# Rows of the first expert pair picked by matmul instead of gathered, in a one-core trunk kernel

## The reference

```python
h = h + moe(rms_norm(h, norm_ffn[i]), ...)
# moe, t = (512, 1024)
g_logits = t @ wg + bg                       # 4 groups
group = argmax(g_logits); p_group = softmax(g_logits)[group]
e_logits = (t @ we + be).reshape(-1, 4, 8)   # 32 experts
top_val, top_idx = top_k(e_logits[group], 2)
gate = softmax(top_val) * p_group            # on the two chosen experts, 0 elsewhere
hid = silu(t @ w1[e]) * (t @ w3[e]) * gate[e]
y  += hid @ w2[e]
```

## Time and profile before

| | |
|---|---|
| median of 3 runs | 1679.25 us (1678.71 to 1692.91) |
| the profiled execution | 1684.34 us |
| its span in the trace | 1682.5 us |
| mean granted clock of PE | 0.966 of full speed |
| busy: PE, DVE, ACT, POOL | 1522.7, 802.8, 419.4, 162.1 us |

### The profile page before, as it was taken

How to read it: one execution, slowest core, us unless ns; L and a number is a source line. 1 busy time by engine, 2 the same in 40 slices (tenths; PEclk the granted TensorE clock), 3 DMA queues, 4 the chain that set the end, 5 groups by cost and what they waited for, 6 DMA issues and landing times.

```text
span 1682.5 us, 29007 instructions
## 1 busy us (share of the span) xinstructions
PE 1522.7 (91%) x12509; PEld 934.8 (56%) x12509; DVE 802.8 (48%) x1403; ACT 419.4 (25%) x849; POOL 162.1 (10%) x183
## 2 busy tenths in 40 slices
PE   6999998889999999699887899999999997988886
PEld 4786777777644864433332378746558545333232
DVE  7655555553754445543221356446643544432125
ACT  2124255454301131400000120027421323000002
POOL 2000223231000000011111200000000001111001
PEclk9999999999999999799999999999999997999898
DMA  8208200011541521579999922220034234999995
GB/s 277 100 1 287 82 4 5 4 48 35 200 150 50 200 100 54 206 295 424 424 425 425 352 84 100 100 100 1 1 128 176 99 114 155 396 425 424 425 407 203
DMA packets 82338, 315.04 MB, mean 187 GB/s; under 512 B 17968, under 2 KB 19048, under 8 KB 57312
## 3 DMA queue, kind: packets, MB, share of 16 engines
q1 hardware_dynamic: 70112, 284.86, 43.6%
q0 software_dynamic: 10944, 24.10, 3.9%
q10 hardware_dynamic: 1152, 4.19, 0.6%
HBM read 306.86 MB, written 34.34 MB: 203 GB/s over the span
## 4 chain that ended last, share of the span: by engine, by line
PE 72%; DMA 14%; DVE 5%; ACT 3%; issue 3%; SPq 2%; PEld 0%; ACTq 0%; DVEq 0%; POOLq 0%
PE PS L790 20%; PE PS L657 13%; DMA arena<-in_moe_w 11%; PE PS L1442 9%; PE PS L2743 7%; PE PS L2768 5%; PE PS L1836 2%; PE PS L1772 2%; PE PS L2692 2%; PE PS L628 2%; PE PS L1812 1%; DMA ring<-in_moe_w 1%; PE PS L2097 1%; PE PS L2118 1%; PE PS L552 1%
## 5 line engine op out<-in xcount | busy, mean ns | idle before, releaser
L790 PE MATMUL PS<-arena,ring 128*128 128x256 f32 x1344 | 299.5, 383 | 2.8 <-DVE arena L934 2.8
L790 PEld LDWEIGHTS PS<-arena,ring 128*128 128x128 f32 x1344 | 255.6, 192 | 42.3 <-issue 6.3
L2743 PE MATMUL PS<-arena 128*64 128x512 f32 x704 | 166.4, 628 | 24.9 <-DMA arena<-in_moe_w 24.9
L657 PE MATMUL PS<-ring,arena 128*128 128x512 f32 x400 | 179.9, 596 | 0.7 <-ACT arena L2063 0.7
L2743 PEld LDWEIGHTS PS<-arena 128*64 128x64 f32 x704 | 52.6, 144 | 136.2 <-issue 103.3
L657 PEld LDWEIGHTS PS<-ring,arena 128*128 128x128 f32 x400 | 74.6, 192 | 83.3 <-issue 82.3
L2751 DVE TENSOR_TENSOR arena<-PS,arena 128x256 f32<-128x256 f32 x32 | 13.6, 424 | 218.6 <-PE PS L2758 201.3
L2748 ACT ACTIVATE arena<-PS 128x256 f32<-128x256 f32 x32 | 12.3, 383 | 327.7 <-PE PS L2743 327.7
L2743 PE MATMUL PS<-ring,arena 128*64 128x512 f32 x320 | 77.0, 637 | 16.1 <-DMA ring<-in_moe_w 12.9
L839 DVE TENSOR_TENSOR arena<-arena,PS 128x512 f32<-128x512 f32 x56 | 36.8, 684 | 112.4 <-PE PS L790 112.4
L1442 PE MATMUL PS<-ring 64*64 64x64 f32 (+1 forms) x3072 | 77.4, 234 | 10.6 <-issue 9.4
(11 more groups left out here) (336 smaller groups left out, 2219.0 us busy)
## 6 DMA issues: line engine op xcount, KB each, us to landing
arena<-in_moe_w SPq DMA_DIRECT2D x120, 1024.0 KB, 20.0
ring<-in_moe_w SPq DMA_DIRECT2D x72, 1024.0 KB, 17.6
ring<-in_sb_wqkv SPq DMA_DIRECT2D x6, 2048.0 KB, 9.2
ring<-in_xa_wq SPq DMA_DIRECT2D x4, 2048.0 KB, 8.6
ring<-in_xa_wo SPq DMA_DIRECT2D x4, 2048.0 KB, 14.2
ring<-in_xa_wkv SPq DMA_DIRECT2D x3, 2048.0 KB, 10.3
h<-in_x SPq DMA_DIRECT2D x8, 512.0 KB, 8.9
ring<-in_rw_wr SPq DMA_DIRECT2D x2, 2048.0 KB, 11.4
```

Of the source, the lines that this page charges most:

```text
L657: ins = pe.matmul(PS[:, BANK_OF[g], :], rows(k), cols[:, k, :], start=(k == 0 and not grows), stop=(k == 3), skip_group_check=grows)
L790: ins = pe.matmul(PS[:, BANK_OF[g], M * c:M * c + M], rows[:, k, o:o + P], cols[:, k, :], start=(c + k == 0 and not grows), stop=(k == 3), ...
L2743: ins = pe.matmul(bank(2, 2, F)[r, :, :], xgT[p][:, k, r], w[a][:, :, k, :], start=(k == 0), stop=(k == KC - 1))
```

## The change

Pair 0's rows are no longer gathered. For each token tile t a 128x128 matrix `picks[t]` is made, one-hot over pair 0's slots and scaled by the token's `rstd`: two `tensor_scalar` and one add. PE multiplies the residual tile `h[:, t, k::KC]` by it, 8 times for the 8 blocks of channels (`pick_tile`), and adds the four tiles up in banks 0 and 3: this gives the rows of pair 0 already turned. DVE scales them into `xgT[0]` (`xgT_first`). POOL makes `picks` for tiles 0, 1 and 2 (`pick_rows`), DVE for tile 3 within `place(3)`. POOL's memsets stand between its tiles 0 and 1. `place(1)` is moved ahead of `second(2)` on DVE. The table is finished later: `filled_table` of tiles 1 to 3 stands between the two halves of `up` of pair 0. POOL's gathers begin with pair 1.

```diff
+            pick_tile(pe, l, 0)
             late_turn(pe, ffn, NT - 1, ready, range(3))
             route_logits(pe, l, NT - 1, ahead)
...
+        def pick_tile(pe, l, t, ks=range(KC)):
+            if t < NT - 1:
+                pe.wait_ge(S("first_picks"), 14 * l + (4, 10, 14)[t])
+            else:
+                pe.wait_ge(S("first_rows"), 3 * l + 1)
+            for k in ks:
+                ins = pe.matmul(bank(PICK_BANKS[k // 4], 4, P)[:, k % 4, :], h[:, t, k::KC], picks[t % 3][:, 0, :],
+                                start=(t == 0 and k % 4 == 0), stop=True, ...)
...
         def moe_route_pe(pe, l):
-            for t in range(NT - 1):
-                filled_table(t)
+            filled_table(pe, l, 0)
+            pick_tile(pe, l, 1)
+            pick_tile(pe, l, 2)
             route_ranks(pe, l, NT - 1)
-            filled_table(NT - 1).then_inc(S("tabled"), 1)
+            pick_tile(pe, l, NT - 1, range(KC // 2)).then_inc(S("first_rows"), 1)
+            for p in range(2):
+                pe.nop().then_inc(S(f"xg_free{p}"), 1)
+            pick_tile(pe, l, NT - 1, range(KC // 2, KC)).then_inc(S("xg_free0"), 1)
+
+        def rest_of_table_pe(pe, l):
+            for t in range(1, NT - 1):
+                filled_table(pe, l, t)
+            filled_table(pe, l, NT - 1).then_inc(S("tabled"), 1)
...
# place(t), on DVE, ahead of OS
+                if t == NT - 1:
+                    own = picks[t % 3]
+                    for k in range(2):
+                        do(vec.tensor_scalar(own[:, k, :], iob, s8[:, NT * k + t:NT * k + t + 1], w_pick[:, k, t:t + 1],
+                                             ALU.is_equal, ALU.mult))
+                    vec.tensor_tensor(own[:, 0, :], own[:, 0, :], own[:, 1, :], ALU.add).then_inc(S("first_rows"), 1)
...
+            place(1)
             second(2)
-            place(1)
             place(2)
...
# POOL
+            def pick_rows(t, before):
+                b, own = 14 * l + before, picks[t]
+                pool.wait_ge(S("onehots"), 28 * l + (4, 6, 9)[t])
+                pool.tensor_scalar(w_pick[:, :, t], OB[:, t, :, 0], rstd[:, t:t + 1], None, ALU.mult)\
+                    .then_inc(S("first_picks"), 1)
+                pool.wait_ge(S("first_picks"), b + 1)
+                for k in range(2):
+                    m = NT * k + t
+                    pool.tensor_scalar(own[:, k, :], iob, s8[:, m:m + 1], w_pick[:, k, t:t + 1], ALU.is_equal, ALU.mult)\
+                        .then_inc(S("first_picks"), 1)
+                pool.wait_ge(S("first_picks"), b + 3)
+                pool.tensor_tensor(own[:, 0, :], own[:, 0, :], own[:, 1, :], ALU.add).then_inc(S("first_picks"), 1)
...
-            for n in range(4):
+            for n in range(1, 4):
                 fetch(n)
...
         def moe_pe(pe, l):
...
                 if n == 0:
-                    pe.wait_ge(S("first_rows"), 2 * l + 2)
+                    pe.wait_ge(S("first_rows"), 3 * l + 3)
                     up(pe, p, 2, w, range(KC // 2))
+                    rest_of_table_pe(pe, l)
                 pe.wait_ge(S("xgT_ready"), NPE * l + n + 1)
...
-            pe.wait_ge(S("table_ready"), l + 1)
-            for p in range(2):
-                pe.nop().then_inc(S(f"xg_free{p}"), 1)
-            turn(0)
```

More of the change, by code:

```diff
@@ L1863, in trunk @@
         XO_SUMS = at(20, [4, 512]), at(15, [4, 2 * P])
+        PICK_BANKS = (0, 3)
         def cross_act(act, l, before):
@@ L2169, in trunk @@
         hidT = at(27.5, [2, P])
+        picks = [at(27, [2, P]), at(27.5, [2, P]), at(26, [2, P])]
         yg = [at(12 + n, [C]) for n in range(8)]
@@ L2204, in trunk @@
         gmax, gsum, v1, v2, s1, ed, den, wA, wB = [c4[:, n, :] for n in range(9)]
+        w_pick = c4[:, 9:11, :]
         bs = masks[:, 4, 64:88].rearrange("p (n t) -> p n t", n=6)
@@ L2300, in route_ranks, with filled_table @@
             pe.matmul(v, ones[:, :], cum[:, t, :], start=False, stop=True).then_inc(S("ranked"), 1)
-        def moe_route_pe(pe, l):
[L2303 to L2308, removed]
-            for t in range(NT - 1):
-                filled_table(t)
-            route_ranks(pe, l, NT - 1)
-            filled_table(NT - 1).then_inc(S("tabled"), 1)
+        def pick_tile(pe, l, t, ks=range(KC)):
[5 more added lines that the diff above has]
+                ins = pe.matmul(bank(PICK_BANKS[k // 4], 4, P)[:, k % 4, :], h[:, t, k::KC], picks[t % 3][:, 0, :],
+                                start=(t == 0 and k % 4 == 0), stop=True,
+                                skip_group_check=not (t == 0 and k % 4 == 0))
+            return ins
+        def filled_table(pe, l, t):
+            pe.wait_ge(S("onehots"), 28 * l + (4, 6, 9, 12)[t])
+            for k in range(2):
+                ins = pe.matmul(PS[:, 5, 0:NPE], OS[:, t, k, :], OB[:, t, k, :], start=(t + k == 0),
+                                stop=(t + k == NT))
+            return ins
+        def moe_route_pe(pe, l):
+            filled_table(pe, l, 0)
+            pick_tile(pe, l, 1)
+            pick_tile(pe, l, 2)
+            route_ranks(pe, l, NT - 1)
+            pick_tile(pe, l, NT - 1, range(KC // 2)).then_inc(S("first_rows"), 1)
[6 more added lines that the diff above has]
+            filled_table(pe, l, NT - 1).then_inc(S("tabled"), 1)
             pe.wait_ge(S("chosen"), 2 * NT * (l + 1))
@@ L2463, in moe_choice_vec @@
             second(3)
+            vec.wait_ge(S("onehots"), 28 * l + 10)
+            do(vec.tensor_scalar(w_pick[:, :, NT - 1], OB[:, NT - 1, :, 0], rstd[:, NT - 1:NT], None, ALU.mult))
             place(3)
@@ L2467, in moe_route_vec @@
             do = stepper(vec, l)
+            vec.wait_ge(S("first_rows"), 3 * l + 2)
+            xgT_first(vec, l, 0).then_inc(S("first_rows"), 1)
+            vec.wait_ge(S("xg_free0"), (NPE // 2 + 1) * l + 2)
+            xgT_first(vec, l, 1).then_inc(S("xgT_ready"), 1)
+            vec.tensor_tensor(gdiff, lg[:, :, 0:G], gmax.unsqueeze(2).to_broadcast([P, NT, G]), ALU.subtract)\
+                .then_inc(S("route_a"), 1)
+            vec.tensor_tensor(ed, v2, v1, ALU.subtract).then_inc(S("route_a"), 1)
             vec.wait_ge(S("tabled"), 9 * l + 1)
@@ L2637, in fetch @@
                 gather(pool, p, P, table[:, n:n + 1]).then_inc(S(f"xg_in{p}"), 16)
+            def pick_rows(t, before):
[4 more added lines that the diff above has]
+                pool.wait_ge(S("first_picks"), b + 1)
+                for k in range(2):
+                    m = NT * k + t
[3 more added lines that the diff above has]
+                pool.tensor_tensor(own[:, 0, :], own[:, 0, :], own[:, 1, :], ALU.add).then_inc(S("first_picks"), 1)
+            pick_rows(0, 0)
             pool.wait_ge(S("proj_filled"), FIRST[f"xo{l}"] + 14)
             for p in range(2):
-                pool.memset(xg[p], 0.0).then_inc(S("xg_cleared"), 1)
-            pool.wait_ge(S("xg_cleared"), 2 * l + 2)
+                pool.memset(xg[p], 0.0).then_inc(S("first_picks"), 1)
+            pick_rows(1, 6)
+            pick_rows(2, 10)
+            pool.wait_ge(S("first_picks"), 14 * l + 14)
             for t in range(2):
@@ L2724, in spread_out, with xgT_first @@
             vec.tensor_copy(gatesT[p].rearrange("p t s -> p (t s)"), PS[:, 3, :]).then_inc(S("gates_last"), 1)
+        def xgT_first(vec, l, b):
+            return vec.tensor_tensor(xgT[0][:, 4 * b:4 * b + 4, :], bank(PICK_BANKS[b], 4, P)[:, :, :],
+                                     gainT[:, GAIN[f"ffn{l}"], 4 * b:4 * b + 4].unsqueeze(2)
+                                     .to_broadcast([P, 4, P]), ALU.mult)
         def turn_rows(pe, p, rows, ks=range(KC)):
@@ L2785, in turn @@
             def turn(n):
[L2786 to L2791, removed]
+                pe.wait_ge(S(f"xg_in{n % 2}"), 16 * ((NPE // 2 - 1 + n % 2) * l + (n + 1) // 2))
+                turn_rows(pe, n % 2, P).then_inc(S(f"xg_free{n % 2}"), 1)
             def up_pair(n):
@@ L2860, in turned @@
             def turned(n):
-                if n == 0:
-                    vec.wait_ge(S("first_rows"), 2 * l + 1)
-                    xgT_out(vec, l, 0, P, (0,)).then_inc(S("first_rows"), 1)
                 vec.wait_ge(S(f"xg_free{n % 2}"), (NPE // 2 + 1) * l + n // 2 + 2)
-                xgT_out(vec, l, n % 2, P, (1,) if n == 0 else range(2)).then_inc(S("xgT_ready"), 1)
+                xgT_out(vec, l, n % 2, P).then_inc(S("xgT_ready"), 1)
             def rows(n):
@@ L2874, in moe_vec @@
             vec.nop().then_inc(S("ye_v"), 1)
-            turned(0)
             for n in range(NPE):
```

3 lines of the change are left out of this document (removed).

## The result

The changed kernel takes 1690.06 us (median of 20 runs, 1681.97 to 1701.20), the kernel before 1681.45 on the same chips (20 runs). The ratio is 1.0052, 95% interval [1.0036, 1.0067]. The prediction was 1669.8 us and a range of 1663 to 1679: the change costs 8.6 us where it was to save 9.4. The profiled execution has a span of 1685.8 us, at a mean granted clock of 0.972 (before: 1682.5 us and 0.966).

A forecast was written before the change was run, and what follows sets the result against it. The experts were taken as bound by a full weight stream starting when pair 0's `up` ends. Per layer 6.2 − 0.5 − 0.6 − 0.3 = 4.8 us (layer 1: 4.6), together 9.4: 1679.25 − 9.4 = 1669.8 us, range 1663 to 1679.

The forecast's parts named there:

- The price of a pick: PE's 16 instructions for one token tile: 0.11 us each at full clock, 1.8 us in all.
- Pick 0: Tile 0's pick in PE's idle 2.68 us before 696.93: 1.8 us, costing nothing if POOL is in time.
- Picks 1 and 2 ahead of the ranks: On PE before tile 3's ranks: hidden at full clock, 3.2 us late at half; taken as 0.5 us.
- pick 3: Tile 3's pick before pair 0's `up`, in two halves of 0.9 us each at full clock or 2.0 at half.
- Pair 1's late gather: Pair 1's gather waits for the table inside pair 0's `up`, opening a stream gap: 0.3 us, bounds 0 and 2.
- The end of the experts follows the start of the stream: In each layer the end moves by the shift of pair 0's `up` end, less any gap in the weights.
- The table: Three tiles and the count on PE inside pair 0's `up`: 1.5 us at full clock, 3.2 at half.
- DVE's path for tile 3: Two one-hots 0.60 us together and an add of some 0.3 ahead of tile 3's pick; 0.95 with handovers.
- the slower rival of 1695: PE's clock stays at half until pair 0's `up` is done: 7.9 us later in each layer, 1695 us; chance 0.06.
- the sum: Net gain of all terms over both layers: 4.8 us in layer 0 and 4.6 in layer 1, together 9.4.
- GpSimd in the way: GpSimd's matrices hold DVE's port and make tile 3's ranks late: gain 2.2 us a layer, 1674.9 us; chance 0.22.
- a GpSimd one-hot: One GpSimd operation with a single input for a tile's pick matrix: 0.30 us, about 1.4 for the tile.

The follow-up runs named there:

- contig: The changed kernel with the picks reading 128 neighbouring channels instead of every 8th, so pair 0's rows hold wrong channels; 1677.51 us, 0.9977 of the kernel before.
- after_table: The changed kernel with the table of tiles 1 to 3 ahead of pair 0's `up` instead of inside it; 1686.47 us, 1.0011 of the kernel before.
- contig_table: The changed kernel with picks from contiguous channels (wrong rows for pair 0) and the table ahead of `up`; 1671.05 us, 0.9919 of the kernel before.
- ct_extra: contig_table plus two small loads of the gain, in 16 pieces of 512 bytes, to an unused tile; 1669.75 us, 0.9934 of the kernel before.
- pool_only: The kernel before, with GpSimd also making the pick matrices of tiles 0 to 2, which nobody uses; 1683.62 us, ratio 0.9992.
- bench: The kernel before with groups of 8 f32 matmuls or transposes added at its end, operands contiguous or stepped; 16 instructions took 1.95 us contiguous, 3.9 at step 8.

## Why the prediction was wrong

**The price of a pick: the step that failed.** "At full clock one is 0.11 us": the 1.8 us of a pick came from the router's and the turning's rows, whose f32 products have contiguous operands or are transposes. The pick reads `h[:, t, k::KC]`, a view with a step of 8 elements, and that is 0.244 us an instruction. The bounds had some 4 us for a pick only where the clock is at half throughout; 3.9 us at full clock was no case at all. The term failed in three places. Pick 0, "nothing", is 3.9 us in an idle stretch of 2.68. Picks 1 and 2 ahead of the ranks, taken at 0.5 with a bound of 3.2, put the ranks of tile 3 2.6 us (layer 0) and 5.1 us (layer 1) later after the router of tile 2 than before; with the short picks of contig they are 1.1 us later and 0.1 earlier. And pick 3, 1.8 us in the saved path, is 4.1 to 4.2. contig gives back 0.75% by this alone.

**Pair 1's late gather: taken at 0.3, bounds 0 and 2.** The mechanism was named, and its size was off: the gaps in the stream are 1.5 us and 3.0 us, the second outside the bounds. In layer 0 `up` of pair 1 starts 4.3 us after `up` of pair 0 has ended (723.12 to 727.43) where it was 2.7 before. In layer 1 `up` of pair 1 is longer as well, at a mean clock of 0.81 (1436 to 1442), behind the idle stretch. Its chain row:

```profile
1435.21 8.59 PE PS L2804 x32
```

Against 7.09 in layer 0 that is 1.5 more, so that the two batches are 1.6 us further apart than before in layer 0 and 3.2 in layer 1. after_table gains 0.4% on the changed kernel by removing it, and contig_table 0.6% on contig; the intervals allow 0.2 to 0.9. The 4.5 us of holes are shown; the ratios moved by 7 and 10 us, and what else moved is not located.

**Right.** The end of the experts follows the start of the stream, less its holes: from the end of `up` of pair 1 to the combination are 221 and 216 us before, 220 and 218 after. The table costs 1.46 us (1.5 forecast). DVE's path for tile 3 is as worked out. The clock came back within a few microseconds in the changed kernel's profile, so that the slower rival of 1695 (chance 0.06) did not happen by its mechanism; that it had the right sign is luck. With both faults out, contig_table gains 13.6 us by its ratio where the sum says 9.4: 0.9919 against 0.9944, at the edge of the interval; ct_extra's 0.9934 [0.9915, 0.9953] takes it in.

**GpSimd in the way (0.22).** pool_only excludes its price: 2 us a layer for the port are 4 in all, and the interval ends at 1.7. The ranks did come late, but by the picks' length. A term was mis-sized here too: a GpSimd one-hot takes 0.80 us, not 0.30, so that a tile's matrix takes 2.4 us rather than 1.4. The Trainium skill's rule ("SBUF — State Buffer", "Who interferes with whom") would block a DVE instruction with two SBUF inputs for all the length of a GpSimd instruction that reads SBUF. The trace does not bear it out: in the changed kernel such a DVE step (L2447, 697.18) took its usual 0.19 us inside the second of two one-hots of 0.80 (696.05 to 697.65), and no DVE step of layer 0 beside a one-hot was made longer by more than the 0.09 of the row above. The memset, which reads nothing, again took L2430 from 0.23 to 0.79, and to that this rule does not apply.

**The range.** It took in the bounds of each term, but all of them rested on one price for a matmul, and none of the rivals varied it. The predicted gain and the loss differ by 18 us. The pick's price is 12.6 of them, and the table's place is worth 7 to 10 by the ratios: both out, contig_table is some 22 us faster than the changed kernel, more than the forecast needs.

## What to carry to other kernels

Price a matmul by a row with the same operand views, not just the same shape: the step of the view belongs to the price. Where no such row is in the trace, the bound should be twice the contiguous one, as measured here, and an order in PE's list that was made for short picks (three places here) should be summed with long ones too. Where transfers are asked for in batches by the end of some work, look at the distance between two such ends against the time one batch lasts: 9.77 against 9.9 us was tight, and anything that went between them came out as a hole. And where a kernel with one more tile is slower in a place that the tile has nothing to do with, compare the stretches ahead of its first use before blaming what it is used for.

## What the hardware showed that I had not expected

- An f32 matmul of 128 columns is 0.12 us an instruction with contiguous operands and 0.13 with a step of 2 elements, and 0.244 with a step of 4 (loaded operand) or 8 (either operand); a transpose from the step 8 view is 0.13 (all in bench).
- A strided pick hardly goes by the granted clock: 3.90 us at 1.00 (691.89), 4.19 in after_table just ahead of the table (708.66), in a stretch at 0.50. The table, contiguous, went from 1.25 us (contig_table) to 2.38 (after_table) between the same two levels.
- Loads were slower in the kernels with one more small tile ahead of their destination: in 20 to 28 us the five kernels with 64 more bytes a partition there have the DMA engines at 1.09 to 1.11 busy for 226 to 238 GB/s, the nine others at 0.93 to 1.06 for 247 to 301. The same five have 420 GB/s rather than 425 in the stream of weights, which the tile may explain and no run isolates.
